# Second feed-forward of a two-block layer: three VectorE operations placed later, and one low part computed on VectorE instead of GpSimd

## The reference, cut to what matters

```python
h = rms_norm(x, norm_mlp[l])
x = x + jnp.square(jax.nn.relu(h @ w_up[l])) @ w_down[l]     # w_up 1024 x 4096, w_down 4096 x 1024
return rms_norm(x, norm_final)
```

## Time and profile before

| what | value |
|---|---|
| median of 3 runs | 2831.03 us (2830.8 to 2833.12) |
| the profiled execution's own time | 2833.39 us |
| its span | 2831.6 us |
| PE busy over the span | 2720.7 us (96%) |
| POOL busy over the span | 1815.9 us (64%) |
| DVE busy over the span | 1793.8 us (63%) |

### The profile page before, as it was taken

How to read it: one execution, slowest core, us unless ns; L and a number is a source line. 1 busy time by engine, 2 the same in 40 slices (tenths; PEclk the granted TensorE clock), 3 DMA queues, 4 the chain that set the end, 5 groups by cost and what they waited for, 6 DMA issues and landing times. The chain is left out here.

```text
span 2831.6 us, 39258 instructions
## 1 busy us (share of the span) xinstructions
PE 2720.7 (96%) x13371; PEld 2245.5 (79%) x13371; DVE 1793.8 (63%) x2179; ACT 1137.7 (40%) x1700; POOL 1815.9 (64%) x1229
## 2 busy tenths in 40 slices
PE   8999998999999999799999999999998999999997
PEld 7888886888888887678878778778786777777786
DVE  5334435556565565676676676667634888988988
ACT  4312316333333333645445355454425434443443
POOL 3333336767777776865555565566326899999993
PEclk9999999999999999899999999999999999999999
DMA  3111111111211212212121121112521121112112
GB/s 122 45 38 37 45 38 30 45 45 47 63 45 51 60 44 75 81 49 60 34 64 48 46 60 49 49 45 64 180 73 30 45 59 46 50 52 59 44 44 97
DMA packets 196117, 160.28 MB, mean 57 GB/s; under 512 B 5719, under 2 KB 176300, under 8 KB 196013
## 3 DMA queue, kind: packets, MB, share of 16 engines
q1 hardware_dynamic: 196013, 158.83, 18.6%
HBM read 143.08 MB, written 15.73 MB: 56 GB/s over the span
## 5 line engine op out<-in xcount | busy, mean ns | idle before, releaser
L340 POOL TENSOR_TENSOR w_lo<-w_raw,w_hi 128x512 fp32r<-128x512 f32 x351 | 503.9, 1443 | 266.8 <-ACT w_hi L334 266.2
L334 ACT CAST w_hi<-w_raw 128x512 fp32r<-128x512 f32 x351 | 211.1, 617 | 399.0 <-DMA w_raw<-in_w_in 113.1
L548 PE MATMUL PA<-h_hi,w_hi 128*128 128x512 f32 x636 | 263.0, 414 | 17.2 <-ACT hy_t L2777 5.6
L549 PE MATMUL PA<-h_lo,w_hi 128*128 128x512 f32 x636 | 251.7, 396 | 0.0
L550 PE MATMUL PA<-h_hi,w_lo 128*128 128x512 f32 x636 | 251.6, 396 | 0.0
L340 POOL TENSOR_TENSOR w_lo<-hy_ring_sums,w_hi 128x512 fp32r<-128x512 f32 x96 | 138.6, 1444 | 67.2 <-ACT w_hi L334 67.2
L340 POOL TENSOR_TENSOR w_lo<-f_sums,w_hi 128x512 fp32r<-128x512 f32 x113 | 174.2, 1542 | 10.3 <-ACT w_hi L334 10.3
L548 PE MATMUL PB<-f_t_hi,w_hi 128*128 128x512 f32 x424 | 169.4, 400 | 9.6 <-ACT hy_tm L2836 5.0
L396 POOL TENSOR_TENSOR w_raw<-w_raw,params 128x1024 f32<-128x1024 f32 x72 | 142.8, 2004 | 45.8 <-DMA w_raw<-in_ffn_w_up 45.8
L550 PE MATMUL PB<-f_t_hi,w_lo 128*128 128x512 f32 x424 | 166.7, 393 | 0.0
L549 PE MATMUL PB<-f_t_lo,w_hi 128*128 128x512 f32 x424 | 166.2, 392 | 0.0
(11 more groups left out here) (664 smaller groups left out, 8417.9 us busy)
## 6 DMA issues: line engine op xcount, KB each, us to landing
w_raw<-in_w_in SPq DMA_DIRECT2D x64, 512.0 KB, 5.1
w_raw<-in_ffn_w_up SPq DMA_DIRECT2D x42, 512.0 KB, 4.8
w_raw<-in_w_down SPq DMA_DIRECT2D x32, 512.0 KB, 3.8
w_raw<-in_w_up SPq DMA_DIRECT2D x30, 512.0 KB, 4.0
w_raw<-in_gla_w_in SPq DMA_DIRECT2D x24, 512.0 KB, 3.7
w_lo_raw<-in_ffn_w_down SPq DMA_DIRECT2D x44, 256.0 KB, 2.6
X<-in_x SPq DMA_DIRECT2D x8, 512.0 KB, 8.4
w_raw<-in_gla_w_out SPq DMA_DIRECT2D x8, 512.0 KB, 3.6
```

Source lines behind the costliest of these rows:

```text
L334: act.copy(self.slot(i, p)[0], source).then_inc(self.hi_done, 1)
L340: pool.tensor_tensor(lo, source, hi.bitcast(F32), ALU.subtract).then_inc(self.split, 1)
L548: pe.matmul(bank, ah[:, k, :], bh[:, k, :], start=(k == 0 and not more), stop=False, skip_group_check=more)
L549: pe.matmul(bank, ah[:, k, :], bl[:, k, :], start=False, stop=False, skip_group_check=more)
```

## The change

The set `LATE` loses P5, so the low part for P5 is no longer made by GpSimd at the end of its round but by VectorE, between the takes of P2 and of P7. The low part for P2, the third sum (A22 less A11 into A11) and the fourth (A12 less A11 into A12) leave `first_blocks`. The first two now stand behind the three additions of `combine`, the last one behind its first subtraction. The order of the counts of `a_sum` and `a_lo` stays as it was, apart from P5 being counted by `a_lo`.

```diff
-        LATE = ('P3', 'P5')
+        LATE = ('P3',)
...
-                def combine(i, between=None):
+                def combine(i, between, behind=None):
...
                     dve.wait_ge(s["u7"], i + 1)
-                    if between:
-                        between()
+                    between()
                     dve.wait_ge(ring.used, ring.done(i, 5))
                     dve.tensor_tensor(W, u22, W, ALU.subtract).then_inc(s["c21"], 1)
+                    if behind:
+                        behind()
                     dve.wait_ge(ring.used, ring.done(i, 6))
                     dve.tensor_tensor(Z, u22, Z, ALU.subtract).then_inc(s["c12"], 1)
...
                     a_low(i, "P7")
+
+                def middle_blocks(i):
+
+                    a_low(i, "P2")
                     dve.wait_ge(s["a_sum"], i * 4 - 3)
                     dve.tensor_tensor(A11, A22, A11, ALU.subtract).then_inc(s["a_sum"], 1)
-                    a_low(i, "P2")
+
+                def last_block(i):
+
                     dve.wait_ge(s["a_sum"], i * 4 - 1)
                     dve.tensor_tensor(A12, A12, A11, ALU.subtract).then_inc(s["a_sum"], 1)
...
                     first_blocks(i)
-                    combine(i)
+                    combine(i, lambda: middle_blocks(i), lambda: last_block(i))
                     take(i, "P1")
                     take(i, "P2")
+                    a_low(i, "P5")
                     take(i, "P7")
                     a_low(i, "P6")
```

## The result

The changed kernel takes 2813.85 us (median of 4; 2812.07 to 2816.69), the kernel before 2830.91 in the same comparison. The medians are 17.1 us apart. The ratio of the runs is 0.9944, with a 95% interval of 0.9929 to 0.9959: faster by 0.56%, some 16 us. The forecast was 2813.0.

What follows compares the result with a forecast made beforehand. TensorE, losing 2.7 us of each 40.78 us round to waits, was to be held by GpSimd's chain at 39.45. One round of 40.1 and 13 of 39.45 make 553.0 against 571.0: 18.0 less, 2813.0 us (range 2805 to 2824).

Steps and rivals of the forecast that it cites:

- The wait at P4 and the fall of the clock go: In `up`, TensorE's 2.24 us loss at P4 and the slow matmuls behind it vanish, with 1.0 us in hand.
- E: Start of the first matmul of the next `up`, put at D + 19.03 us.
- The three moved operations cost nothing: Behind the additions of `combine`, VectorE's idle time covers them, with 0.2 us to spare at the end.
- The price of an operation on two SBUF tiles: VectorE waits out GpSimd's current operation plus half a microsecond; GpSimd's next one starts work 0.48 us late.
- GpSimd's chain sets the round at 39.45: GpSimd's 40.24 us round loses 1.25 for P5's low part and gains 0.48: 39.45, which TensorE's round comes to equal.
- f: Time from D to the start of P3's low part on GpSimd, forecast to settle at 4.0 us.
- The round as f + 35.45: TensorE's round when P5's and P6's low parts wait for GpSimd in `down`, delaying the fifth product; 39.45 us at f = 4.0.
- D: Start of the first matmul of `down` in a round, from which the forecast counts times.
- W: Start of GpSimd's scalings in a round, put at D + f + 1.25 us.
- Rival 1: P5's move gains GpSimd nothing; the stall moves from P4 into `down`, rounds of 40.2, 8 us less, 2823; chance 0.20.
- Rival 2: The two low parts meet gaps of GpSimd; its chain of 39.0 binds, 25 us less, 2806; chance 0.15.
- Rival 3: Slower: both low parts meet GpSimd at its worst in `down`, the clock falls, rounds of 42.1, 2849; chance 0.07.

Runs made afterwards that it cites:

- gp_extra: The changed kernel with one more GpSimd operation of 128x512 a round, ahead of GpSimd's wait for ScalarE: 2817.84 us, 0.9952 of the kernel before.
- scale_halves: The changed kernel with each GpSimd scaling split into two operations of 128x512: 2816.88 us, 0.9949 of the kernel before.
- p6_later: The changed kernel with P6's low part behind the takes of P3 instead of ahead of them: 2815.45 us, 0.9954 of the kernel before.
- p5_only: The kernel before with only P5's low part moved to VectorE, the three operations left ahead of the additions: 2823.97 us, 0.9974 of the kernel before.
- rows_first: The changed kernel with ScalarE making the first two down rows' high parts ahead of its copy of `u22`: 2817.58 us, 0.9960 of the kernel before.
- moves_only: The changed kernel with P5's low part back on GpSimd, so only the three operations are moved: 2824.5 us, 0.9980 of the kernel before.
- no_scaling: The changed kernel with GpSimd's two scalings cut to 16 columns each, other up weights left unscaled: 2801.8 us, 0.9905 of the kernel before.

## Why the prediction was right, step by step

- **The wait at P4 and the fall of the clock go.** Right, in size too: second addition at E + 11.8, 1 us ahead of need, no restart and no matmul at 0.43. That the clock falls behind waits of 2 us was too plain: in the kernel before, P4 was 2.2 us late in 7 rounds, and the clock fell in 4 of them.
- **The three moved operations cost nothing.** Right: the last subtraction comes 0.2 behind `down`'s first matmul, as before, with 0.3 us or more idle ahead of it in every round (the forecast had 0.2).
- **The price of an operation on two SBUF tiles**, what is left of GpSimd's operation and half a microsecond, held everywhere (0.47 to 0.54 behind its end): 2453.28 lies in the second scaling, which ends about 2454.6, and the next take starts at 2455.06.
- **GpSimd's chain sets the round at 39.45.** Half right. In 6 of 13 rounds the scalings are 39.36 to 39.49 apart, as forecast. In the other 7 they are 39.74 to 39.81 apart, because of a path that the forecast left out: from VectorE's low part for P7 over ScalarE's copy and first row's high part to GpSimd. In the timeline, GpSimd's L340 starts at 2473.89, E + 9.8. The next scaling starts 16.2 later at about 2490.1, which puts P3's low part at f = 5.7 of the next round. Nor is the chain rigid: the 1.3 us of gp_extra cost 0.26. But GpSimd is never far from being the bound, since in scale_halves and p6_later, which let TensorE go, the round was short twice and back at 39.5 to 40 from the third one on.
- **The round as f + 35.45, and with it f = 4.0.** This step failed. It is right where f is below 5.05, the 6.30 at which P5's low part is due less the 1.25 of P3's on GpSimd (p5_only 40.33 against 40.40, rows_first 39.78 against 39.7 to 39.8), and not the case of this kernel. At f = 5.5 P5's low part is due (D + 6.30) while GpSimd still makes P3's low part. It goes ahead as that ends and costs 0.96 (2449.93 to 2450.89), where the formula has it wait for the whole first scaling. The first scaling then bears the 0.48 (it starts at 2450.37, and the second ends later), and P6's low part waits for the second scaling: 1.78 (2453.28 to 2455.06), not 1.4; its length of 1.85 lies outside the 1.2 to 1.5 that the forecast named as a sign. With the next take 0.51 behind the second scaling, W + 4.22 + 0.51, the fifth product stands at D + f + 6.71, and the round is f + 34.01: 39.5 for 5.5, 39.8 for 5.75. The rounds of D = 2443.63 and 2483.16, with f of 5.48 and 5.71, took 39.53 and 39.77. On this line the forecast's own chain of 39.45 gives f = 5.44: f was missed by the formula, and only by 0.25 in 7 rounds through ScalarE.
- **The sum** of 18.0 us came out as 16.9 in the profiles and 17.1 between the medians. The first round took 39.2 in place of 40.1, the others 39.6 in the mean in place of 39.45. The wrong f did not spoil the sum, since the round came from GpSimd's chain and f only had to fit it. That it did not is partly luck: a round of 39.45 fits both formulas, at f = 4.0 and at f = 5.44, but at 5.0, just below the border, the first one gives 40.45, and p5_only, at 4.9, took 40.40. rows_first, at f = 4.3 and 39.75, looks like the state that was forecast; it entered the loop with f = 3.62, the full change with 5.06. Whether that decides between the two was not tested.
- **The rivals.** Rival 1, GpSimd gaining nothing from P5's move, falls. moves_only shows what its chain would have cost, and the difference to the full change is 8.7 us of the stage. The Trainium skill (Perfetto Trace Analysis, Optimizing Scalar/DVE Operations) says that such a move might not help. Here it did, P5's move alone bringing 0.26%. The reason that the page gives, the shared port, is seen in the trace: 2.3 us a round came back as waits in `down`. Rival 2's condition (low parts that meet no scaling) was made in no_scaling: 543.2 us for the stage, where 546 was the estimate. But that run also spares GpSimd 3.3 us a round, so the nearness proves little. Rival 3 did not occur. The wait at the fifth product is 1.3 at most, with the clock full.

The two parts together gave 16.9 us of the stage, alone 8.2 and 5.4. By the ratios it is 0.56% against 0.20% and 0.26%, and with intervals that reach 0.08 to 0.15% to either side it is not shown that together they give more than their sum. What the traces show is what each leaves behind alone: the moves a late GpSimd (f about 8), P5's move a phase of 4.9, at which P5's low part meets the scaling.

## What to carry to other kernels

Where VectorE works on two SBUF tiles beside a busy GpSimd, the price of an operation is set by what GpSimd is doing at that moment, 0.68 to 2.35 us long here for the same 128x512. So count the phase, not only the work, and look for the long GpSimd operations first. An engine that is busy for most of a round need not bind it: add one operation ahead of its longest wait and see whether the time moves. Read every round before building on a wait of one: the 1.76 us that GpSimd waits here stand in 7 rounds of 13. When a stage loops over several engines that each have a microsecond to spare, removing one wait makes the next; compare with the bare time of the engine that must not wait (38.07 us a round here) to know when to stop.

## What the runs showed of the hardware

- A VectorE operation of 128x512 on two SBUF tiles took 0.68 us beside an idle GpSimd and up to 2.35 beside a busy one; the operation behind it started 0.47 to 0.54 us after the end of the GpSimd operation under way, and GpSimd's next one then took about 0.45 longer (2.35 for 1.90, 1.74 for 1.29). Two engines that both have such work take turns, 1.70 us a pair.
- Takes (one operand in PSUM) that followed each other without a wait took 0.60 us from start to start beside a busy GpSimd, and 0.60 beside an idle one (25 cases in no_scaling).
- A shift of GpSimd's phase by 0.6 us (f 4.9 in p5_only, 5.5 in the full change) goes with a loss of TensorE in `down` of 1.5 us a round in place of 2.3. The port goes to whichever is first: in p5_only the scaling, and P5's low part is 2.29 us long; in the full change the low part, 1.04 us long. The Trainium skill (SBUF — State Buffer, SBUF: two separate sides) says that whichever of the two starts first holds the shared pair for its whole instruction, and the traces agree with it.
- The clock of TensorE fell behind 4 of 7 waits of 2.2 us in the kernel before (0.427 us a matmul in place of 0.227), and behind none of those of 1.1 to 1.3 us in the kernel after, nor of those of up to 1.8 us in p6_later.
